# A hybrid S5 / dilated / forgetting attention block: the state-space inputs u made with stationary weights and turned by transposes

## What is computed

```python
h = rms_norm(x, g_pre_mix[l])
proj = h @ w_in[l]
u_ssm, qkv_dsa, qkv_fox, f_logit = jnp.split(proj, offsets, axis=-1)   # u: 256 columns, f_logit: 6
...
y_ssm = s5_mixer(u_ssm, ...)
log_f = jax.nn.log_sigmoid((f_logit + b_f[l]).astype(jnp.float32))
y_fox = forgetting_attention(q * scale, k, v, log_f)
```

## Time and profile before

| | us |
|---|---|
| median of 3 runs | 1375.34 (1374.59 to 1377.39) |
| the profiled execution | 1376.55, of which the span of the trace is 1374.9 |
| PE busy | 1312.2 (95% of the span), 6812 matmuls |
| DVE busy | 562.4 (41%) |
| ACT busy | 431.1 (31%) |
| POOL busy | 334.9 (24%) |
| PE's share of the chain that ended last | 87% |

### The profile page before, as it was taken

One profiled execution on the slowest core, in us unless ns is written; L12 is line 12 of the kernel. 1 busy time (PEld: TensorE's weight loads), 2 busy tenths in 40 slices (PEclk: granted clock), 3 DMA queues, 4 the chain that ended last, 5 costly groups with the idle time before them and its releaser, 6 DMA issues.

```text
span 1374.9 us, 18319 instructions
## 1 busy us (share of the span) xinstructions
PE 1312.2 (95%) x6812; PEld 1119.6 (81%) x6812; DVE 562.4 (41%) x1093; ACT 431.1 (31%) x842; POOL 334.9 (24%) x313
## 2 busy tenths in 40 slices
PE   7999999996999997999999999999999999999996
PEld 7999888885888885888878888888888888888885
DVE  7271545245777776575231122112211211121137
ACT  6232222145777773353203101210121022103222
POOL 6019622132555520000202200410031022102300
PEclk9999999998999998999999999999999999999998
DMA  5013343148456521134111102110211031002042
GB/s 192 31 64 84 127 113 138 61 133 240 95 139 138 149 55 61 46 93 138 46 77 46 47 15 92 46 46 0 92 56 36 0 107 46 31 14 109 16 153 108
DMA packets 41601, 112.73 MB, mean 82 GB/s; under 512 B 16534, under 2 KB 16582, under 8 KB 39612
## 3 DMA queue, kind: packets, MB, share of 16 engines
q1 hardware_dynamic: 36252, 95.15, 20.3%
q0 software_dynamic: 5296, 16.87, 6.5%
HBM read 87.27 MB, written 24.14 MB: 81 GB/s over the span
## 4 chain that ended last, share of the span: by engine, by line
PE 87%; issue 5%; DVE 3%; ACT 2%; POOL 2%; DMA 2%; SPq 0%; DVEq 0%; ACTq 0%; POOLq 0%
PE ps L1899 17%; PE ps L1882 11%; PE ps L1883 11%; PE ps L1884 11%; PE ps L1857 6%; PE ps L384 3%; PE ps L385 3%; PE ps L386 3%; PE ps L1768 2%; PE ps L1658 2%; PE ps L1660 2%; PE ps L1659 2%; PE ps L1752 1%; PE ps L1626 1%; PE ps L1627 1%
## 5 line engine op out<-in xcount | busy, mean ns | idle before, releaser
L1882 PE MATMUL ps<-op_hi,w_hi 128*128 128x512 f32 x704 | 274.1, 389 | 1.6 <-DVE ol L937 1.6
L1884 PE MATMUL ps<-op_hi,w_lo 128*128 128x512 f32 x704 | 273.9, 389 | 0.0
L1883 PE MATMUL ps<-ol,w_hi 128*128 128x512 f32 x704 | 273.9, 389 | 0.0
L1417 POOL TENSOR_TENSOR hid_lo<-hf,hid_hi 128x512 fp32r<-128x512 f32 x44 | 56.9, 1293 | 683.1 <-ACT hid_hi L888 683.1
L1882 PEld LDWEIGHTS ps<-op_hi,w_hi 128*128 128x128 f32 x704 | 132.1, 188 | 29.2 <-DVE ol L937 1.8
L1884 PEld LDWEIGHTS ps<-op_hi,w_lo 128*128 128x128 f32 x704 | 132.1, 188 | 27.5
L1883 PEld LDWEIGHTS ps<-ol,w_hi 128*128 128x128 f32 x704 | 132.1, 188 | 27.3
L366 DVE TENSOR_TENSOR w_lo<-w_raw,w_hi 128x1024 fp32r<-128x1024 f32 x44 | 57.9, 1315 | 212.8 <-ACT w_hi L361 212.8
L882 ACT ACTIVATE tg<-ps 128x512 f32<-128x512 f32 x44 | 26.4, 599 | 367.0 <-PE ps L1884 367.0
L937 DVE TENSOR_TENSOR z<-ps,z 128x512 f32<-128x512 f32 x80 | 51.6, 686 | 142.8 <-PE ps L1899 142.4
L1899 PE MATMUL ps<-wd_hi,hid_hi 128*128 128x512 f32 x352 | 108.5, 389 | 1.4 <-POOL hid_lo L1417 1.4
(11 more groups left out here) (267 smaller groups left out, 2510.4 us busy)
## 6 DMA issues: line engine op xcount, KB each, us to landing
w_raw<-w_stream SPq DMA_DIRECT2D x56, 512.0 KB, 3.3
wd_raw<-w_down SPq DMA_DIRECT2D x5, 2048.0 KB, 9.9
qk_scratch<-qk_hi SPq DMA_DIRECT2D x12, 512.0 KB, 2.6
qk_scratch<-qk_lo SPq DMA_DIRECT2D x12, 512.0 KB, 2.9
qa<-qk_scratch POOLq DMA_DIRECT2D x24, 256.0 KB, 4.2
ks<-qk_scratch POOLq DMA_DIRECT2D x24, 256.0 KB, 5.5
xt<-x_t SPq DMA_DIRECT2D x8, 512.0 KB, 7.0
wo_raw<-w_out SPq DMA_DIRECT2D x4, 1024.0 KB, 5.0
```

The costliest lines, as they stand in the source:

```text
L1417: return pool.tensor_tensor(out, a, b, op)
L1882: pe.matmul(out, w2_hi[:, j, k, :], op_hi[:, k, half(h)], start=k == 0, stop=False)
L1883: pe.matmul(out, w2_hi[:, j, k, :], ol[:, k, half(h)], start=False, stop=False)
L1884: last = pe.matmul(out, w2_lo[:, j, k, :], op_hi[:, k, half(h)], start=False, stop=k == KT - 1)
```

## The change

The product for u alone is turned round: the weights are stationary (two tiles n of 128 columns), x moves in runs of 512 tokens, so it is 2 x 2 x 8 x 3 = 96 matmuls of 512 columns. They fill banks 0 to 3. ACT copies the four banks into a new tile `ud` (channels on partitions). After the second V tile `u_transposed` turns it on PE: 16 transposes of 128x128, whose stationary operand is `ud` with a step of 8, two token sets to a bank. ACT then copies the four banks to `ug`. The forget weights come by a transfer of their own (`f_raw`) and are columns 256 to 261 of V's first third, whose matmuls have 262 columns; ACT copies f out at each m, scaled by the token's norm, and the transposes of `fl` read tokens in plain order. The token sums go to the end of bank 7; V's tiles m < 4 no longer wait for u's copies, m == 3 waits for DVE to have read the sums, m == 4 for the last copy of u.

```diff
             for k in range(KT):
...
-                    sync.dma_start(uf_raw[:, k:k + 2, :], w_uf[:, k:k + 2, :]).then_inc(uf_in[k // 2], 16)
+                    sync.dma_start(u_raw[:, k:k + 2, :], w_u[:, k:k + 2, :]).then_inc(uf_in[k // 2], 16)
             sync.dma_start(bc[:], s_bc).then_inc(bc_in, 16)
             sync.dma_start(bfs[:], b_f).then_inc(bc_in, 16)
+            sync.dma_start(f_raw[:], w_f).then_inc(bc_in, 16)
...
+            act.wait_ge(bc_in, 16 * 3)
+            act.activation(vh[:, 0, :, VW:VF], f_raw[:], ACT.Copy)
             v_high(0)
 
             act.wait_ge(uf_mm, 1)
-            act.activation(fl[:], ps[:, :, SSM_W:UF], ACT.Copy).then_inc(uf_copied, 1)
-            for s in (4, 5, 6, 7, 0, 1, 2, 3):
-                act.activation(ug[:, :, s, :], ps[:, s, 0:SSM_W].rearrange("p (g c) -> p g c", c=CH),
-                               ACT.Copy).then_inc(uf_copied, 1)
+            act.wait_ge(sq_added, KT - 1)
+            for k in range(SSM_W // P):
+                for h in range(2):
+                    act.activation(ud[:, k, half(h)], ps[:, 2 * k + h, :], ACT.Copy).then_inc(uf_copied, 1)
             rsqrt_act(act, n1s_norm, rn[:, 0, :], rn[:, 1, :])
+            for b in range(TS // 2):
+                act.wait_ge(ud_mm, b + 1)
+                act.activation(ug[:, :, 2 * b:2 * b + 2, :].rearrange("p g t c -> p t g c"),
+                               ps[:, b, :].rearrange("p (t g c) -> p t g c", t=2, c=CH), ACT.Copy).then_inc(uf_copied, 1)
...
+                    if w == 0:
+                        act.activation(fl[:, m, :], ps[:, 4 + m % 4, VW:VF], ACT.Copy, scale=rn[:, 0, m:m + 1])
...
             def v_low(w):
                 dve.wait_ge(v_high_done, w + 1)
-                tt(vl[:, w % 2, :, :], v_raw, vh[:, w % 2, :, :].bitcast(f32), ALU.subtract).then_inc(v_split, 1)
+                if w == 0:
+                    tt(vl[:, 0, :, VW:VF], f_raw[:], vh[:, 0, :, VW:VF].bitcast(f32), ALU.subtract)
+                tt(vl[:, w % 2, :, 0:VW], v_raw, vh[:, w % 2, :, 0:VW].bitcast(f32), ALU.subtract).then_inc(v_split, 1)
...
-            for s in range(TS):
-                pe.matmul(ps[:, s, 0:UF], op_hi_c[:, 0, s, :], ufh[:, 0, :], start=True, stop=False)
+            U_TILES = [(n, slice(n * P, (n + 1) * P)) for n in range(SSM_W // P)]
+            for n, cols in U_TILES:
+                for h in range(2):
+                    pe.matmul(ps[:, 2 * n + h, :], uh[:, 0, cols], op_hi[:, 0, half(h)], start=True, stop=False)
             for k in range(KT):
                 pe.wait_ge(x_split, k + 1)
                 pe.wait_ge(uf_split, k // 2 + 1)
-                for s in range(TS):
-                    out = ps[:, s, 0:UF]
-                    if k:
-                        pe.matmul(out, op_hi_c[:, k, s, :], ufh[:, k, :], start=False, stop=False)
-                    pe.matmul(out, op_hi_c[:, k, s, :], ufl[:, k, :], start=False, stop=False)
-                    last = pe.matmul(out, op_lo_c[:, k, s, :], ufh[:, k, :], start=False, stop=k == KT - 1)
+                for n, cols in U_TILES:
+                    for h in range(2):
+                        out = ps[:, 2 * n + h, :]
+                        if k:
+                            pe.matmul(out, uh[:, k, cols], op_hi[:, k, half(h)], start=False, stop=False)
+                        pe.matmul(out, uh[:, k, cols], op_lo[:, k, half(h)], start=False, stop=False)
+                        last = pe.matmul(out, ul[:, k, cols], op_hi[:, k, half(h)], start=False, stop=k == KT - 1)
             last.then_inc(uf_mm, 1)
 
+            def u_transposed():
+
+                pe.wait_ge(ident_set, 1)
+                pe.wait_ge(uf_copied, 2 * SSM_W // P)
+                for t in range(TS):
+                    for n, cols in U_TILES:
+                        at = (t % 2) * SSM_W + n * P
+                        last = pe.transpose(ps[:, t // 2, at:at + P], ud_c[:, n, t, :], ident[:])
+                    if t % 2:
+                        last.then_inc(ud_mm, 1)
+
...
                 for m in range(NT):
-                    if w == 0 and m < 4:
-
-                        pe.wait_ge(uf_copied, 2 + m)
                     if w == 0 and m == 1:
                         token_sums()
+                    if w == 0 and m == 2:
+                        u_transposed()
+                    if w == 0 and m == 3:
+                        pe.wait_ge(n1s_norm.mean, 1)
                     if w == 0 and m == 4:
+                        pe.wait_ge(uf_copied, 2 * SSM_W // P + TS // 2)
                         for h in range(2):
                             norm_sums(pe, n1_norm, acc1, 0, h)
...
-                    out = ps[:, 4 + m % 4, 0:VW]
+                    n = VW if w else VF
+                    out = ps[:, 4 + m % 4, 0:n]
```

More of the change, by code:

```diff
@@ L46 @@
 PARTS = (2, 4, 4, 4, 4, 4)
-UF = SSM_W + NH
 VW = 256
+VF = VW + NH
 NV = 2 * ATT_W // VW
@@ L84, in __init__, with block_kernel @@
         self.seed = sem(name + "_seed")
-def block_kernel(nc, x_t, x_tok, gains, gain_rows, w_uf, w_v, w_stream, w_out, w_down, s_par, s_bc, rows,
+def block_kernel(nc, x_t, x_tok, gains, gain_rows, w_u, w_f, w_v, w_stream, w_out, w_down, s_par, s_bc, rows,
                  w_glu, b_f, lnc_dram, out_t):
@@ L119, in block_kernel @@
         w_high, w_split, mm_done, evacuated = (sem(n) for n in ("w_high", "w_split", "mm_done", "evacuated"))
+        ud_mm = sem("ud_mm")
         x_high, x_split, sq_x, sq_added, uf_high, uf_split, uf_mm, uf_copied, uf_scaled = (sem(n) for n in (
@@ L203, in block_kernel @@
         r2 = region("hidden_region", 64 * KB,
-                    [("ufh", [P, KT, UF], f32r), ("ufl", [P, KT, UF], f32r), ("uf_raw", [P, KT, UF], f32),
-                     ("acc1", [P, SEQ], f32), ("vh", [P, 2, KT, VW], f32r), ("vl", [P, 2, KT, VW], f32r)],
+                    [("uh", [P, KT, SSM_W], f32r), ("ul", [P, KT, SSM_W], f32r), ("u_raw", [P, KT, SSM_W], f32),
+                     ("acc1", [P, SEQ], f32), ("vh", [P, 2, KT, VF], f32r), ("vl", [P, 2, KT, VF], f32r)],
                     [("dre", [P, NJ, TS + 1, CH], f32), ("dim", [P, NJ, TS + 1, CH], f32),
@@ L218, in block_kernel @@
                     [("last_row", [P, D], f32), ("last_junk", [P, D], f32)])
-        ufh, ufl, vh, vl, uf_raw, acc1 = (r2[n] for n in ("ufh", "ufl", "vh", "vl", "uf_raw", "acc1"))
+        uh, ul, vh, vl, u_raw, acc1 = (r2[n] for n in ("uh", "ul", "vh", "vl", "u_raw", "acc1"))
         dre, dim_, ere, eim, ut, tz, mt, mb, pt, wg, row = (r2[n] for n in
@@ L238, in block_kernel @@
             ("xt", "vst", "hs", "qk_hi", "qk_lo", "qko", "yn", "fz", "ya", "xr", "xu", "z"))
-        r4 = region("chunk_region", 24 * KB + 4 * TS * UF + 64,
+        r4 = region("chunk_region", 24 * KB + 4 * TS * (SSM_W + NH) + 64,
                     [("w_hi", [P, 2, KT, P], f32r), ("w_lo", [P, 2, KT, P], f32r), ("w_raw", [P, 2, KT, P], f32),
-                     ("ug", [P, G, TS, CH], f32), ("fl", [P, TS, NH], f32)],
+                     ("ug", [P, G, TS, CH], f32), ("fl", [P, NT, NH], f32)],
                     [("sq1", [P, 2, SEQ], f32), ("n1", [P, 2, SEQ], f32)],
+                    [("ud", [P, SSM_W // P, SEQ], f32)],
                     [("wo_lo", [P, KT, D], f32r)],
@@ L247, in block_kernel @@
                     [("skip_wd", [P, 16 * KB], mybir.dt.uint8), ("wd_raw", [P, 4, D], f32)])
-        w_hi, w_lo, w_raw, ug, fl, sq1, n1, wo_lo, wo_raw, wd_hi, wd_lo, wd_raw = (r4[n] for n in (
-            "w_hi", "w_lo", "w_raw", "ug", "fl", "sq1", "n1", "wo_lo", "wo_raw", "wd_hi", "wd_lo", "wd_raw"))
+        w_hi, w_lo, w_raw, ug, fl, sq1, ud, n1, wo_lo, wo_raw, wd_hi, wd_lo, wd_raw = (r4[n] for n in (
+            "w_hi", "w_lo", "w_raw", "ug", "fl", "sq1", "ud", "n1", "wo_lo", "wo_raw", "wd_hi", "wd_lo", "wd_raw"))
         r5 = region("row_region", 4 * KB, [("rb", [P, SEQ], f32)], [("post_row", [P, D], f32)])
@@ L272, in block_kernel @@
         bfs = sb("bfs", [NH, 1])
+        f_raw = sb("f_raw", [P, KT, NH])
         ps = ctx.enter_context(nc.psum_tensor("ps", [P, 8, HALF], f32))
@@ L288, in block_kernel @@
         op_hi_c = op_hi[:].rearrange("p k (c t) -> p k t c", t=TS)
-        op_lo_c = op_lo[:].rearrange("p k (c t) -> p k t c", t=TS)
+        ud_c = ud[:].rearrange("p k (c t) -> p k t c", t=TS)
         ol_c = ol[:].rearrange("p k (c t) -> p k t c", t=TS)
@@ L309, in ssm_bank @@
             return ps[:, 4 + n, :].rearrange("p (t c) -> p t c", t=4)
+        sums_bank = ps[:, 7, HALF - 2 * NT:HALF]
         def att_bank(lo, hi, bank):
@@ L668, in _ @@
                     act.wait_ge(uf_in[k // 2], 16)
-                    act.activation(ufh[:, k:k + 2, :], uf_raw[:, k:k + 2, :], ACT.Copy).then_inc(uf_high, 1)
+                    act.activation(uh[:, k:k + 2, :], u_raw[:, k:k + 2, :], ACT.Copy).then_inc(uf_high, 1)
                 if k >= 2:
@@ L995, in input_matrix @@
             def input_matrix():
-                dve.wait_ge(bc_in, 32)
+                dve.wait_ge(bc_in, 16 * 3)
```

(29 more changed lines are left out.)

8 lines of the change are left out of this document (3 added, 5 removed).

## The result

| | before | after |
|---|---|---|
| median | 1375.34 us (5 runs, 1374.58 to 1377.39) | 1364.99 us (5 runs, 1364.13 to 1372.5) |
| ratio, 95% interval | | 0.9926 (0.9912 to 0.9941) |
| span of the profiled execution | 1374.9 | 1370.8 |

The change saves 10.4 us. Measured again, each time beside the kernel before, it took 1364.95 us against 1375.82 (e1), 1365.2 against 1375.71 (e11), and with an addition that costs nothing 1364.13 against 1375.35 (e9) and 1364.8 against 1375.71 (e12). The head of the kernel, where the change is, did not lose it: the first chunk of q starts at 126.90 in this trace, at 126.75 and 126.17 in the other two of the same kernel (e1, e11).

The account below looks back on a forecast made before the run. The prediction took u to be bound by strided weight loads on PE's path. Its terms, -13.0 + 0.5 + 3.8 + 1.4 = -7.3 us, gave 1368.0 us from the median 1375.34, with a range of 1364.5 to 1371.5 plus 1 us.

Parts of the forecast that it names:

- The bound: In u, strided loads of the stationary operand set PE's pace: 192 matmuls at 0.243 us, 46.66 us on the path.
- u now waits for DVE, V's start is 42.1: u's faster matmuls wait for DVE's low parts; V starts at 42.1 instead of 55.12, -13.0 us.
- The clock in u's gaps: Rival: PE's granted clock falls while it waits in u; total -6.0, 1369.3 us; chance 0.17.
- The rival's costly case: A clock fall in u's last burst: 13 matmuls lose 2.6 us, 1.3 of it covered by V's wait.
- The rival "slower": Short bursts in u never bring the clock up; u ends at 49.8, total +3.6, 1379 us; chance 0.03.
- The columns, +0.5: V's first third: 192 matmuls have 6 more columns at 0.0026 us each, +0.5 us.
- The transposes, +3.8: 16 strided transposes of u ahead of V's tile 2, priced like the strided token sums, +3.8 us.
- rival "packed pace": u's transposes go at the pace of packed ones; total -9.4, 1366.0 us; chance 0.06.
- The clock behind the transposes, +1.4: V's tile 2 runs at a lowered clock after u's transposes, as tile 1 did behind the token sums, +1.4 us.
- Nothing behind V: After V all waits follow one another and move as a whole; at most 0.1 us in DVE's first step on f.
- later falls: Clock falls later in the kernel, coming at another moment; 1 us of the range was allowed for them.

Follow-up runs that it names:

- e1: The changed kernel once more, unchanged: 1364.95 us against 1375.82 for the kernel before.
- e11: The changed kernel a third time, unchanged: 1365.2 us against 1375.71 for the kernel before.
- e9: The changed kernel with three unused 512-column products in PE's idle 0.8 us ahead of the 64-partition state-space products: 1364.13 us against 1375.35 before.
- e12: The kernel of e9 again, on the same chip as e11: 1364.8 us against 1375.71 for the kernel before.
- e3: The kernel before, with u's stationary operand 128 neighbouring tokens instead of a step of 8: 1362.32 us, ratio 0.9903 to before.
- e6: The changed kernel with DVE making V's first low part ahead of the small steps of coefficient(): one execution of 1364.38 us.
- e4: The changed kernel with u's 16 transposes reading neighbouring tokens instead of a step of 8: transposes 1.79 us, no total given.
- e5: The changed kernel with u's 16 transposes replaced by ordinary 128-column matmuls with the same strided stationary operand, in fp32r: 1373.53 us.
- e2: The kernel before once more, unchanged, to see how much its trace varies: 1374.17 us.

## Why the prediction was right, step by step

- **The bound.** u was bound by strided loads of its stationary operand: shown by e3. The rule of the Trainium skill that counts columns ("TensorE: Matmul & The Clock Gate", "Back-to-back issue gap") would have had no gain; the run says -13.3 us at V's start. The same section gives that rule for a single matmul in isolation and says that in a stream of loads and matmuls both set the spacing, which is what e3 shows. The note on cachelines in "SBUF — State Buffer" agrees with e3 for an ordinary load.
- **u now waits for DVE, V's start is 42.1.** It was 41.78, with PE idle ahead of k = 2, 3 and 6. The step to PE was 0.05 instead of 0.2, the small subtraction 0.12 instead of 0.2, and DVE ran 0.06 earlier: -13.3 instead of -13.0. e6 shows that DVE's order set it, by 0.8 us and not by 1.3.
- **The clock in u's gaps.** The rival had a fall in the early gaps absorbed by the wait until 35.31, and so it was: two falls, nothing lost. The last burst ran at 1.00. The rival's costly case, a fall in the last burst, did not come in this trace; it came in e4, where it cost V's start 0.7 us of the 1.3 that the rival had. So that nothing was lost here is a matter of the moment. (The rival "slower" adds 24.0 and five tiles of 5.1 to 49.8; it is 49.5, which changes nothing.)
- **The columns, +0.5: too small.** A tile of 24 matmuls of 262 columns took about 0.1 us more, 0.7 over the seven tiles beside tile 1, where the sum had 0.5 for eight. The thirds with 256 columns also cost 0.5 more, and DVE's second step on f 1.77 us instead of 1.49; neither was in the sum, which had a small gain in DVE's first step (it stayed 1.27). Together +1.5 instead of +0.5.
- **The transposes, +3.8: wrong by half.** The step that failed is the choice of the nearest row. I took the strided half of the token sums, because step and columns of the load were the same, over the packed transposes of the earlier trace rows. e5 shows that the kind of operation decides: +1.9, close to the packed end of the range. This was the rival "packed pace", to which I gave 0.06.
- **The clock behind the transposes, +1.4: wrong.** Tile 2 ran at full clock in every trace, also in e5 with loads as slow as I had assumed. The side of the strided u stage was the right one. (With tile 1's full 4.38 us the term would have been 1.55.) In its place tile 1 ran at the lower level to its end, +1.0, which I had put at no change: before, the clock had come back after three quarters of it. This term is a matter of the moment in part: with the sums unchanged, tile 1 of the changed kernel took 5.4 us in six traces, 4.81 in e11 and 4.43 in e5, that of the kernel before 4.38 and 4.62 (e2). Why it is mostly longer after the change was not found.
- **Nothing behind V.** The waits moved along as a whole, in e1 against e2 to 0.2 us. The 1.4 us that the medians have on top are not explained for certain; the clock in the state-space products, one of the "later falls" for which I had widened the range by 1 us, would fit. In the first trace of after it cost 6.

So -7.3 was -13.3 + 1.5 + 1.9 + 1.0 = -8.9 in the head. The mechanism, strided loads as the bound and DVE as the next one, was right. The two terms that I had priced from the token sums were 3.3 us too dear, and that tile 1, V and f cost 2.0 us more than I had said hid more than half of it. That is luck: without it the time would have lain below the range, whose lower end (1364.5) the 1364.99 us only just clears.

## What to carry to other kernels

Look at the mean of the weight loads beside the mean of the matmuls: where a load of 128 columns takes 340 ns instead of 190 and the matmuls follow each other at 0.24 us, the step of 8 in the ordinary loads is the bound. Here it was worth 13 us to take it out, with the same number of matmuls (e3) as with half of them. A float32 transpose takes the step at no visible cost in its pace, so it is the place for it; it is also a cheap way to bring sums over partitions to DVE (1.7 us for 16 instead of 5.5, and the clock stays up). When PE gets faster than the splits that feed it, the order of small steps on DVE is worth time too, 0.8 us here.

## What the runs showed of the hardware that I had not expected

- A strided load of the stationary operand costs 333 to 339 ns in an ordinary matmul and 192 in a float32 transpose, against 192 and 141 packed.
- The granted clock can fall in a stretch of 64-partition products that keeps PE busy: 14 us at 0.50 and 6 us lost in the first trace of after, none in two other traces of the same kernel (e1, e11).
- 3.6 us of strided loads with 128 columns each kept the clock at 1.00 (e5), the 5.5 us of token sums with one column each took it down in all eleven traces that have them.
- One-column sums in float32 showed as two rows with a load each (8 sums, 16 rows), a float32 transpose as one.
